# Rows of a mixture-of-experts block dealt over 16 lanes, and two blocks of 96 slots in place of 128

## What is computed

```
lg = (xt @ router_w_group) + router_b_group          # 4 groups, the best one is taken
le = (xt @ router_w_expert) + router_b_expert        # 8 experts in it, the best two are taken
top_l, top_i = lax.top_k(le, TOP_K)
wts = p_grp[:, None] * jax.nn.softmax(top_l, axis=-1)
...
h = jax.nn.silu(xb @ w_gate[e]) * (xb @ w_up[e])     # 1024 -> 512
yb = (h @ w_down[e]) * w[:, None]                    # 512 -> 1024
y = y.at[slot_tok].add(yb)                           # each token gets two experts' rows
```

## Time and profile before

| | us |
|---|---|
| median of 3 runs | 1716.95 |
| lowest and highest | 1715.2, 1720.86 |
| profiled execution | 1711.8 |
| its span | 1710.0 |
| TensorE busy in the span | 1642.7 (96%) |
| VectorE, ScalarE, GpSimd busy | 661.3, 339.4, 163.9 |
| mean DMA rate in the span | 197 GB/s |
| granted TensorE clock, mean | 0.98 |

### The profile page before, as it was taken

One profiled execution on the slowest core, in us unless ns is written; L12 is line 12 of the kernel. 1 busy time (PEld: TensorE's weight loads), 2 busy tenths in 40 slices (PEclk: granted clock), 3 DMA queues, 4 the chain that ended last, 5 costly groups with the idle time before them and its releaser, 6 DMA issues.

```text
span 1710.0 us, 22521 instructions
## 1 busy us (share of the span) xinstructions
PE 1642.7 (96%) x9285; PEld 1009.8 (59%) x9286; DVE 661.3 (39%) x1395; ACT 339.4 (20%) x670; POOL 163.9 (10%) x169
## 2 busy tenths in 40 slices
PE   7999999999999999999999999999999999999990
PEld 5556777777777666666688555654444444444440
DVE  1446464544542323232477745551111212121225
ACT  1113222323231221222122000101111111111115
POOL 1000000000002422111000000001111111111110
PEclk9999999999999999999999999989999999999995
DMA  7201121121027445443263443289999999999975
GB/s 229 62 18 24 50 63 50 52 61 50 13 75 210 170 148 172 140 136 112 65 235 125 187 160 136 101 302 390 391 392 377 392 395 391 381 389 396 389 268 203
DMA packets 104410, 337.67 MB, mean 197 GB/s; under 512 B 24378, under 2 KB 68482, under 8 KB 87924
## 3 DMA queue, kind: packets, MB, share of 16 engines
q1 hardware_dynamic: 89572, 276.22, 43.0%
q0 software_dynamic: 13568, 55.78, 10.8%
q10 hardware_dynamic: 1168, 4.23, 0.6%
HBM read 307.90 MB, written 35.51 MB: 201 GB/s over the span
## 4 chain that ended last, share of the span: by engine, by line
PE 91%; DMA 5%; DVE 2%; issue 1%; ACT 1%; POOL 0%; SPq 0%; DVEq 0%; POOLq 0%; ACTq 0%
PE psum L1075 12%; PE psum L1189 10%; PE psum L1515 8%; PE psum L1520 7%; PE psum L1377 6%; PE psum L1392 5%; PE psum L1541 4%; PE psum L1116 4%; PE psum L1547 4%; PE psum L979 3%; PE psum L1228 3%; PE psum L1089 2%; DMA arena<-in_w_up 2%; PE psum L1134 2%; PE psum L1528 2%; PE psum L1123 2%
## 5 line engine op out<-in xcount | busy, mean ns | idle before, releaser
L1075 PE MATMUL psum<-arena 128*128 128x258 f32 x896 | 215.3, 384 | 0.0
L1189 PE MATMUL psum<-arena 128*128 128x344 f32 x576 | 182.3, 458 | 0.0
L1075 PEld LDWEIGHTS psum<-arena 128*128 128x128 f32 x896 | 162.9, 190 | 27.9 <-issue 7.0
L1520 PE MATMUL psum<-arena 128*64 128x512 f32 x320 | 141.6, 595 | 0.0
L1521 PE MATMUL psum<-arena 128*64 128x512 f32 x320 | 141.6, 595 | 0.0
L1515 PE MATMUL psum<-arena 128*128 128x512 f32 x320 | 139.8, 595 | 1.1 <-DVE arena L2552 1.1
L1189 PEld LDWEIGHTS psum<-arena 128*128 128x128 f32 x576 | 103.3, 190 | 52.9 <-issue 11.2
L1515 PEld LDWEIGHTS psum<-arena 128*128 128x128 f32 x320 | 60.0, 190 | 73.6 <-issue 73.2
L1377 PE MATMUL psum<-arena 128*128 128x258 f32 x448 | 99.9, 387 | 0.9 <-ACT arena L1802 0.9
L1392 PE MATMUL psum<-arena 128*128 128x512 f32 x224 | 99.2, 596 | 0.0
L1377 PEld LDWEIGHTS psum<-arena 128*128 128x128 f32 x448 | 86.6, 194 | 14.3 <-issue 1.3
(11 more groups left out here) (394 smaller groups left out, 2125.6 us busy)
## 6 DMA issues: line engine op xcount, KB each, us to landing
arena<-in_w_gate SPq DMA_DIRECT2D x32, 2048.0 KB, 24.7
arena<-in_w_up SPq DMA_DIRECT2D x32, 2048.0 KB, 30.3
arena<-in_w_down SPq DMA_DIRECT2D x32, 2048.0 KB, 30.6
arena<-in_w_in SPq DMA_DIRECT2D x33, 512.0 KB, 5.3
gates<-arena SPq DMA_DIRECT2D x16, 516.0 KB, 6.1
arena<-gates SPq DMA_DIRECT2D x16, 516.0 KB, 6.6
arena<-in_x_prompt SPq DMA_DIRECT2D x16, 512.0 KB, 4.5
arena<-in_w_o SPq DMA_DIRECT2D x1, 4096.0 KB, 17.6
```

What stands on the lines that cost most here:

```text
L1075: ins = mm(psum[:, BANK[name[0]], 0:QT], held, moved, start=(k == 0 and name in ("X1", "V6", "Y5")), stop=(k == 3), skip_group_check=True)
L1189: ins = mm(psum[:, FB + t, 0:SP3], wring[:, u, k, :], xT[:, k, t * SP3:(t + 1) * SP3], start=(k == 0), stop=(k == KD - 1))
L1520: g = mm(psum[0:64, 2, :], xgT[:, xpar, k, 0:64], wg[:, k, :], start=(k == 0), stop=(k == KD - 1))
```

## The change

Three things are changed. First, ranks under `FIXED` count as 96-slot blocks, so blocks 0 and 1 go by the code of a 96-slot block on every engine. Second, the rows of a block are dealt: with `each` = slots / 16, the row of position j in block of rank b goes to slot `lane * each + j // 16`, where `lane = (j + b // 2) % 16`. So each sixteenth of a block's slots holds at most one row more than another. Third, VectorE computes these slots: the slots-per-lane figure travels in the upper bits of the slot code (`CODE`), some small instructions are added, and the six instructions on `r_t`, `r_d` and `d_f` now stand ahead of `rows_right(0)`.

```diff
-        row_i2, blk_i = z(2, NT), z(2, NT)
-        row_f2, blk_f = z(2, NT), z(2, NT)
+        part_i, part_f = z(4, 2, NT), z(4, 2, NT)
+        turned, row_f2 = z(2, NT), z(2, NT)
...
+        LANES, CODE = 16, 1 << 13
...
         def full(n):
-            return RANK[n] < FULL
+            return FIXED <= RANK[n] < FULL
 
         def three(n):
-            return FULL <= RANK[n] < MID
+            return RANK[n] < FIXED or FULL <= RANK[n] < MID
...
-            link(nc.vector.tensor_scalar(iota_1, iota_f, 1.0, None, ALU.add))
+            link(nc.vector.tensor_scalar(iota_1[:, 3 * P // 4:P], iota_f[:, 3 * P // 4:P], 1.0, None, ALU.add))
+            link(nc.vector.tensor_scalar(iota_1[:, 0:3 * P // 4].rearrange("p (g j) -> p g j", g=LANES), iota_f[:, 0:3 * P // 4].rearrange("p (j g) -> p g j", g=LANES), 1.0, None, ALU.add))
...
                 link(ts(out, by, float(FULL), None, ALU.is_lt))
+                link(stt(out=out, in0=by, scalar=float(FIXED), in1=out, op0=ALU.is_ge, op1=ALU.mult))
...
             width(cap, rank)
+            link(stt(out=rank, in0=cap, scalar=float(CODE // (P * LANES)), in1=rank, op0=ALU.mult, op1=ALU.add))
...
-            rows_right(0)
             link(tt(r_t, r_t, over_t(skip), ALU.mult))
             link(tt(r_d, r_d, r_t, ALU.add))
             for k, m in enumerate((m1, m2)):
                 link(tt(r_t, r_d, m, ALU.mult))
                 link(nc.vector.tensor_reduce(d_f[:, k, :], r_t, AX_X, ALU.add))
-            link(nc.vector.tensor_copy(slot_of.bitcast(I32), d_f))
-            link(ts(row_i2.bitcast(I32), slot_of.bitcast(I32), P - 1, None, ALU.bitwise_and))
-            link(nc.vector.tensor_copy(row_f2, row_i2.bitcast(I32)))
-            link(tt(blk_f, d_f, row_f2, ALU.subtract))
+            rows_right(0)
+            slot_i = slot_of.bitcast(I32)
+            each, lane, layer, of_blk = (part_i[:, q].bitcast(I32) for q in range(4))
+            link(nc.vector.tensor_copy(slot_i, d_f))
+            ts(each, slot_i, CODE.bit_length() - 1, None, ALU.logical_shift_right)
+            ts(layer, slot_i, P - 1, LANES.bit_length() - 1, ALU.bitwise_and, ALU.logical_shift_right)
+            ts(of_blk, slot_i, CODE - P, None, ALU.bitwise_and)
+            link(ts(turned.bitcast(I32), slot_i, (2 * P).bit_length() - 1, None, ALU.logical_shift_right))
+            link(tt(turned.bitcast(I32), turned.bitcast(I32), slot_i, ALU.add))
+            link(ts(lane, turned.bitcast(I32), LANES - 1, None, ALU.bitwise_and))
+            link(nc.vector.tensor_copy(part_f, part_i.bitcast(I32)))
+            link(tt(row_f2, part_f[:, 1], part_f[:, 0], ALU.mult))
+            link(tt(row_f2, row_f2, part_f[:, 2], ALU.add))
+            blk_f = part_f[:, 3]
```

More of the change, by code:

```diff
@@ L511, in build @@
         FIRST = 1 << 16
+        LANES, CODE = 16, 1 << 13
+        assert NBLK * P <= CODE
         assert T * NE < FIRST
         def full(n):
-            return RANK[n] < FULL
+            return FIXED <= RANK[n] < FULL
         def three(n):
-            return FULL <= RANK[n] < MID
+            return RANK[n] < FIXED or FULL <= RANK[n] < MID
         def room(n):
@@ L2533, in _ @@
             link(nc.vector.tensor_copy(total, psum[:, 2, 1:NE + 1]))
-            link(stt(out=skip, in0=psum[:, 2, 0:NE], scalar=float(NE), in1=rank, op0=ALU.add, op1=ALU.subtract))
+            link(stt(out=skip, in0=psum[:, 2, 0:NE], scalar=float(NE + CODE // LANES), in1=rank, op0=ALU.add, op1=ALU.subtract))
             link(stt(out=skip, in0=skip, scalar=float(P), in1=cap, op0=ALU.mult, op1=ALU.subtract))
```

## The result

Both kernels ran 22 times, side by side. The changed kernel takes 1719.96 us (1713.29 to 1724.53), the one before 1715.40 us (1708.76 to 1722.87). The ratio is 1.0026, with a 95% interval of 1.0016 to 1.0035: some 4.5 us slower. Forecast were 1711.0 us and a range of 1704 to 1718, so the time lies outside the range and on the other side of no change. The forecast was built on 1716.95 us, the median of 3 runs of the kernel before; in differences it was -5.9 us, the kernel lost 4.5, and the miss is 10.4 us. The profiled execution of the changed kernel has a span of 1716.2 us, against 1710.0 before.

What follows compares the result with a forecast made beforehand. TensorE and the DMA engines were both full in mid-mixture, with TensorE deciding the chain until the last additions. Front -4.6, clock +1.7, block 27's wait -1.5 and end -1.5 gave -5.9, from 1716.95 to 1711.0 us; range 1704 to 1718.

Steps and rivals of the forecast that it cites:

- The 9.7 us of TensorE: Blocks 0 and 1 at 96 slots: gate, up and down products save 9.7 us of TensorE's time, not all arriving.
- The gap: Ahead of the slot tables: TensorE idles 4.5 us for VectorE's tables behind block 0's late gate; slot tables start +1.5 us.
- The clock in the gap: Behind TensorE's idle time ahead of the slot tables: a short clock fall costs +1.7 us, bounds 0 and +5.1.
- rival 4: Behind the idle time ahead of the slot tables: the long clock fall, +5 for +1.7, 1714.4 us; chance 0.10.
- rival 1: Ahead of the slot tables: the clock stays up, 1709.3 us, or 1707.9 with even shares; chance 0.26.
- The start of block 0: Ahead of block 0: added VectorE instructions cost +0.2 us, bounds 0 and +1, for a start at 1121.9.
- What dealing gives: Weight stream: fullest DMA engine relieved by 24 us, or 14 by the page's layout; weights stay ahead, -1.5 us.
- rival 3: Weight stream: dealing relieves nothing, TensorE's lead is given back, late requests cost up to +3.7; 1718 to 1720.7 us; chance 0.10.
- Rival 2: 128-slot tiles: an engine serves two groups of four partitions; end -0.4, 1712.1 us, or 1710.4 with clock up; chance 0.14.
- The wait of block 27: Late in the mixture: TensorE's 1.48 us wait for weights at block 27 goes, -1.5 us.
- The end: Additions of the last blocks: dealing shortens block 28's by 1.1 us and block 29's by 0.4, -1.5 us.

Runs made afterwards that it cites:

- tables first: Changed kernel with block 0's gate product on VectorE moved behind the one-hot tables that the slot tables wait for: 1714.37 us, ratio 0.9984 to the kernel before.
- the filler: Changed kernel with seven useless products of 384 columns in TensorE's queue ahead of the slot tables: 1717.42 us, ratio 1.0001 to the kernel before.
- dealt by groups of four: Kernel before with dealing alone, 128-slot blocks dealt by groups of four partitions, blocks 0 and 1 kept at 128 slots: 1711.84 us, ratio 0.9972.
- narrow blocks alone, tables first: Kernel before with only blocks 0 and 1 at 96 slots, block 0's gate product moved behind the one-hot tables: 1719.50 us, ratio 1.0011.
- either repair: Changed kernel with block 0's gate product behind the one-hot tables (0.9984), or with 128-slot blocks dealt by groups of four partitions (0.9970).
- both gate places let go late: Kernel before, with the matrices replacing blocks 0 and 1's gate matrices requested only after that block's up product: 1720.55 us, ratio 1.0019.
- narrow blocks alone: Kernel before with only blocks 0 and 1 at 96 slots, no dealing: 1723.07 us, ratio 1.0041.

## Why the prediction was wrong

- **The 9.7 us of TensorE** were right within 0.7: with tables first the requests show 4.6 + 4.4 = 9.0.
- **The gap** was right in its cause and size: 4.47 us for 4.5, slot tables 16.2 us behind block 0 for 16.1.
- **The clock in the gap** was mis-sized. I took +1.7 out of 0 to +5.1, "as short as the first"; the slot tables alone take 4.0 us more (8.72 against 4.68), and the filler gives 4.3 back. This is +2.6, and the ratio of the filler is uncertain by about as much; the 8.72 is read from one trace. It was rival 4 (0.10), and rival 1, a clock that stays up, is refuted.
- **The start of block 0** was right in what the change does to it (0.3 us more of wait for 0.2) and not in what happened: 4.1 us later in the trace by a longer fall of the clock. Whether the dealing makes that fall likelier the runs don't settle. Block 0 starts 3.2 to 8.3 us later than in before's trace in seven of the eight profiles with dealing, and in none of the four others without it, where it is -1.7 to +2.0 us. But the profiled executions of these four, and of the eighth with dealing (dealing alone, +1.1 us), are among the three fastest of their kernels, and before's is a fast one too; and over its 12 runs the kernel with the dealing alone has a mean clock of 0.979 in the median, before beside it 0.977. A kernel with the long fall in its profile, dealt by groups of four, is still 0.28% faster than before.
- **What dealing gives is the step that failed.** "What is needed is only 4.6 us and 1.5 us. So weights stay ahead" has two errors. What was needed was more: the requests that the narrow block delays I had found, with +3.7 us, and had put only into rival 3, as if a relief of 6 us paid for them. Requests late by 6.9 us, nearly twice as much, cost 3.3 to 4.8 us with nothing else changed, and the lead of TensorE comes on top. And what was given was less: 2.1 to 4.6 us by the pairs of kernels, against 14 us by groups of four partitions (24 by sixteenths). Why 32 rows less on an engine give so much less than 32 x 0.43 us stays open. The price of a row isn't the likely error, since 15 rows less by groups of four gave 6.8 us for 6.5; it may be the count of rows, which takes sixteenths as the shares of the tiles of 96, 64 and 32 slots. No run tested those tiles, and none measured the fullest engine itself.
- **Rival 2**, the groups of four in a tile of 128, is what the runs bear out. I gave it 0.14 and priced only the end with it (-0.4 in place of -1.5), since 14 us seemed ample. The runs put 4.5 to 9.6 us on it.
- **The wait of block 27** goes with the dealing alone, as forecast (-1.5). In the changed kernel the waits are 4.9 us.
- **The end**: block 28's addition took 12.69 for 13.09 and block 29's 5.30 for 6.18. A kernel without dealing has 11.95 and 5.57 (narrow blocks alone, tables first), so not even this is the dealing's for certain. The -1.5 us isn't shown.
- **Rival 3** gave 1718 to 1720.7 us, and the time is 1719.96. That it lies inside is partly luck: the base has come down by 1.6 us since, and as a difference rival 3 gave +3.7 at most for 4.5 measured. Its mechanism holds by half: dealing relieves something, but the late requests and the given-back lead are as it says, and the clock's loss makes up the sum. A chance of 0.10 was too low for a case whose condition, relief under 6 us, hung on the one thing that I had no row for, the layout of the shares.

Of the miss, 4.5 - (-5.9) = 10.4 us, a run measured +2.6 as the clock of the gap. The other 7.8 us lie with the stream, and no run parts them: the late requests (3.3 to 4.8 us for a delay longer than the form of block 0 makes, but in the changed kernel more requests are late, by the gap), and the lead of TensorE that I had counted as kept. That it is given back the traces show (with tables first from 4.4 us ahead to 6.2 behind); what each of the two is worth in the time of the changed kernel stays open. With either repair the sign turns (0.9984 and 0.9970), so neither of them alone had to lose.

## What to carry to other kernels

When two resources are full at once, price a faster step on both: what it takes off the engine, and at what time it frees the buffers for the next transfers. A request that comes 7 us late while the DMA engines have room is paid for 400 us later. A form of a product that frees two buffers together at its end can ask for the next transfer later than a longer one that frees the first halfway, here by 3.6 us. And before rows are spread over DMA engines, find out which partitions an engine serves: the same dealing with other groups was 4.5 to 9.6 us apart.

## What the hardware showed

- The clock falls behind waits for weights, too, and the fall costs 1.3 to 2.9 us beyond the wait: 64 products of 3.66 us take 5.35 behind waits of 2.22, 3.24 and 3.30 us, 5.78 behind one of 4.81, 5.00 behind one of 3.83 (with the filler) and 6.54 behind one of 4.56 (narrow blocks alone, tables first). Behind waits of 0.62 to 1.71 they take 3.66. Two waits of nearly one length came out differently. With both gate places let go late,

```profile
1557.96 3.66 PE L1530 MATMUL psum<-arena 128*32 128x256 f32 x64 [1.89 <-DMA arena<-in_w_up]
```

and with the narrow blocks alone

```profile
1452.38 5.30 PE L1528 MATMUL psum<-arena 128*32 128x256 f32 x64 [1.86 <-DMA arena<-in_w_up]
```

- One kernel's executions differ in the clock by themselves, and the time goes with it: of the 29 of before that stand beside the first experiments, one of 1712.06 us has a mean granted clock of 0.979 and one of 1720.08 us has 0.974. The profiled execution of before, 1711.8 us at 0.980, is at that favourable end. The difference of the two profiled spans, 6.2 us, therefore overstates the 4.5 of the medians, and differences to before's trace can hold some of this, the start of block 0 above all.
